# The delta rule's output gate: projected token tile by token tile from both halves of a side

## The reference

```python
def gated_deltanet_mixer(h, w_in, conv_w, a_log, dt_bias, out_norm, w_out):
    proj = h @ w_in                                     # [512, 1024] @ [1024, 4112]
    qkv = causal_depthwise_conv_silu(proj[..., :o1], conv_w)
    z = proj[..., o1:o2].reshape(b_sz, t_len, GDN_HEADS, GDN_DV)
    ...
    o = gated_delta_rule_chunked(q, k, v, g, beta).astype(h.dtype)
    o = rms_norm(o, out_norm) * jax.nn.silu(z)
    return o.reshape(b_sz, t_len, GDN_V_WIDTH) @ w_out
```

## Time and profile before

| | us |
|---|---|
| median of 3 runs | 2427.6 |
| lowest and highest | 2426.79, 2427.78 |
| the profiled execution | 2430.54 |
| its span in the trace | 2428.8 |

### The profile page before, as it was taken

The page is one execution under the profiler, slowest core; times in us unless marked ns, Lnnn a source line. Parts: engine busy times, 40 slices in busy tenths (PEclk is TensorE's granted clock), DMA queues, the critical chain, the costliest instruction groups (busy, mean ns, idle before and its releaser), DMA issues. The chain is left out here.

```text
span 2428.8 us, 26752 instructions
## 1 busy us (share of the span) xinstructions
PE 2238.0 (92%) x10932; PEld 1765.1 (73%) x10932; DVE 1128.3 (46%) x1668; ACT 811.1 (33%) x1147; POOL 138.3 (6%) x52
## 2 busy tenths in 40 slices
PE   6998899989999997999597899999899898999997
PEld 4885467868878875787495688888678566888885
DVE  2014765633254266876564544431552545544413
ACT  4311374333133154443133332221332653322211
POOL 3331000000000001310010000000000000000000
PEclk9997899999999998999688999999999999999998
DMA  3311002222223222232202223222234012222321
GB/s 126 104 57 53 1 1 70 96 81 93 99 75 105 87 70 72 72 109 92 65 23 70 69 87 104 87 95 96 69 105 156 1 53 70 89 102 87 104 87 52
DMA packets 43015, 190.22 MB, mean 78 GB/s; under 512 B 15808, under 2 KB 16512, under 8 KB 22032
## 3 DMA queue, kind: packets, MB, share of 16 engines
q1 hardware_dynamic: 40560, 184.32, 22.2%
q10 hardware_dynamic: 2336, 4.23, 0.5%
HBM read 184.80 MB, written 3.74 MB: 78 GB/s over the span
## 5 line engine op out<-in xcount | busy, mean ns | idle before, releaser
L422 PE MATMUL psum<-split,weights_high 128*128 128x512 f32 x1688 | 680.6, 403 | 54.1 <-DVE split L1160 19.5
L424 PE MATMUL psum<-split,weights_low 128*128 128x512 f32 x1688 | 676.1, 401 | 0.0
L423 PE MATMUL psum<-split,weights_high 128*128 128x512 f32 x1688 | 674.1, 399 | 0.0
L240 DVE TENSOR_TENSOR weights_low<-weights_raw,weights_high 128x2048 fp32r<-128x2048 f32 x139 | 318.6, 2292 | 563.9 <-ACT weights_high L213 563.8
L213 ACT CAST weights_high<-weights_raw 128x2048 fp32r<-128x2048 f32 x164 | 309.8, 1889 | 588.7 <-PE psum L424 580.9
L422 PEld LDWEIGHTS psum<-split,weights_high 128*128 128x128 f32 x1688 | 321.8, 191 | 139.7 <-issue 26.0
L423 PEld LDWEIGHTS psum<-split,weights_high 128*128 128x128 f32 x1688 | 322.0, 191 | 77.9
L424 PEld LDWEIGHTS psum<-split,weights_low 128*128 128x128 f32 x1688 | 321.1, 190 | 79.0 <-issue 0.2
L230 POOL TENSOR_TENSOR weights_low<-weights_raw,weights_high 128x2048 fp32r<-128x2048 f32 (+3 forms) x25 | 108.2, 4329 | 862.4 <-ACT weights_high L213 855.3
L424 PE MATMUL psum<-hidden,weights_low 128*128 128x512 f32 x352 | 140.4, 399 | 0.0
L423 PE MATMUL psum<-hidden,weights_high 128*128 128x512 f32 x352 | 138.7, 394 | 0.0
(11 more groups left out here) (406 smaller groups left out, 2703.2 us busy)
## 6 DMA issues: line engine op xcount, KB each, us to landing
weights_raw<-in_weights SPq DMA_DIRECT2D x161, 1024.0 KB, 4.8
minus_c<-minus_c_rows ACTq DMA_DIRECT2D x16, 256.0 KB, 7.5
x_stream<-in_x SPq DMA_DIRECT2D x2, 1024.0 KB, 7.9
gdn_in_grown<-gdn_rows SPq DMA_DIRECT2D x4, 512.0 KB, 4.5
gdn_chain_grown<-gdn_rows SPq DMA_DIRECT2D x4, 512.0 KB, 4.1
out<-x_stream SPq DMA_DIRECT2D x8, 256.0 KB, 2.1
rope_table<-rope_tables SPq DMA_DIRECT2D x1, 1024.0 KB, 5.3
weights_raw<-in_weights SPq DMA_DIRECT2D x1, 768.0 KB, 4.2
```

What stands on the lines that cost most here:

```text
L240: self.nc.vector.tensor_tensor(out=self.low[:, n % 2, 0:width], in0=self.raw[:, n % 2, 0:width], in1=self.high[:, n % 2, 0:width].bitcast( ...
L422: nc.tensor.matmul(bank, wh, ah, start=first, stop=False)
L423: nc.tensor.matmul(bank, wh, al, start=False, stop=False)
L424: return nc.tensor.matmul(bank, wl, ah, start=False, stop=last)
```

## The change

PE takes both chunks of a side together: it waits once for the second chunk's low part, and then runs the 24 matmuls of token tile 0, of tile 1, and so on. The number of matmuls, their operands and shapes stay. `products` counts two for each tile at its end, where it counted one for each half. ACT's `split_high` of +2 and +4 move from behind tile 0 to behind tile 3, with an explicit wait for the last tile. DVE's `split_low_vector` of +2 moves from behind tile 0 to behind the five solve steps of tile 3, right before that of +3.

```diff
             def gate_done(side, j):
-                return weights.tiles_before[z_chunk + 2 * side + 1] + j + 1
+                return weights.tiles_before[z_chunk + 2 * side] + 2 * (j + 1)
...
                         for side in range(2):
-                            for half in range(2):
-                                chunk = z_chunk + 2 * side + half
-                                pe.wait_ge(weights.low_ready, chunk + 1)
-                                parts = weights.parts(Chunk(chunk), 4)
-                                for j in range(TT):
-                                    if half == 0:
-                                        if side == 0:
-                                            pe.wait_ge(bank_free, n_tiles - 3 + j)
-                                        else:
-                                            pe.wait_ge(z_read, j + 1)
-                                    for k in range(4):
-                                        a = 4 * half + k
-                                        token = [split[:, n, a, j * P:(j + 1) * P] for n in range(2)]
-                                        last = product(psum[:, j, :], token, [p[:, k, :] for p in parts], a == 0, a == DT - 1)
-                                    last.then_inc(weights.products, 1)
+                            first = z_chunk + 2 * side
+                            pe.wait_ge(weights.low_ready, first + 2)
+                            for j in range(TT):
+                                if side == 0:
+                                    pe.wait_ge(bank_free, n_tiles - 3 + j)
+                                else:
+                                    pe.wait_ge(z_read, j + 1)
+                                for a in range(DT):
+                                    parts = weights.parts(Chunk(first + a // 4), 4)
+                                    token = [split[:, n, a, j * P:(j + 1) * P] for n in range(2)]
+                                    last = product(psum[:, j, :], token, [p[:, a % 4, :] for p in parts], a == 0, a == DT - 1)
+                                last.then_inc(weights.products, 2)
...
                                 nc.scalar.activation(tanh[:, o % 2, :], psum[:, j, :], ACT.Tanh, scale=0.5).then_inc(tanh_ready, 1)
-                                if j == 0:
-                                    weights.split_high(act, Chunk(z_chunk + 2 + 2 * side))
+                            act.wait_ge(weights.products, gate_done(side, TT - 1))
+                            weights.split_high(act, Chunk(z_chunk + 2 + 2 * side))
                             if side == 0:
                                 weights.split_high(act, Chunk(z_chunk + 3))
...
                                 if side == 0 and j == 0:
-                                    weights.split_low_vector(dve, z_chunk + 2)
                                     dve.wait_ge(col_pe, 3)
...
-                            weights.split_low_vector(dve, z_chunk + 3 + side)
+                            weights.split_low_vector(dve, z_chunk + 2 + 2 * side)
+                            if side == 0:
+                                weights.split_low_vector(dve, z_chunk + 3)
```

## The result

| | before | changed |
|---|---|---|
| median of 6 runs, us | 2427.69 (2426.79 to 2429.9) | 2439.02 (2437.0 to 2439.24) |
| profiled execution, us | 2430.54 | 2438.99 |
| its span, us | 2428.8 | 2437.0 |

The change makes the kernel slower: ratio 1.0042, 95% interval 1.0029 to 1.0055, that is +7.0 to +13.4 us. Timed again later it was 2436.96 against 2428.25 us, ratio 1.0032 (1.0021 to 1.0043), +8.7 us. Forecast were +5.4 us and 2430.4 to 2436.6 us. The sign was right, the size was not.

A forecast was written before the change was run, and what follows sets the result against it. DVE's queue was taken to set the stage's end. Start +4.1, turn +5.5, restarts -1.8, small terms -0.3 and tail -2.2 gave +5.3 (+5.4 by the stage's end), so 2433.0 us; range 2430.4 to 2436.6 us.

The forecast's parts named there:

- Bound of the kernel: Gate stage: DVE's queue up to the transposed copy's end sets the end, 1185.53 us before; PE does not.
- Step 1: Start of side 0: PE also waits for the second chunk's low part and starts 4.1 us later.
- Step 2: DVE in side 0: first tile 4.1 us earlier, at 1133.5; the gain is spent waiting for tiles.
- Step 3, the turn: Between the sides: PE stands 11.0 us for high parts, DVE's solves and two low parts; before, 2.49 + 2.99.
- Step 4: PE's side 1: 22.49 us of matmuls plus 1.9 for the restart, ending at 1185.3 against 1177.7 before.
- Step 5: Tail: high part, low part and copy end 5.65 us behind PE, 7.8 before; 2.2 us come back.
- What is not in the trace: When the clock rises later, in the next stage: taken as 0, with 1.5 us on either side.
- From the profile to the median: The stage's whole shift carried on to the median: 2427.6 + 5.4 = 2433.0 us, 0.22% more.
- B (faster): DVE's queue alone sets the end and its earlier start brings it 4.1 us forward: 2423.5 us; chance 0.03.
- A: Cheap restarts and a shorter low clock stretch next stage: +3.2 us, 2430.8, no change that can be told; chance 0.30.
- C: Restart after 11 us of rest takes much longer at 1.2 GHz: +8.1 us, 2435.7; chance 0.07.

The follow-up runs named there:

- pad_tail: The kernel before, with five more transposed copies of the solved blocks in DVE's tail: +6.8 us against before.
- solve_early: The kernel before, half by half, with 15 solve steps moved into DVE's idle time ahead of tile 0 and its other work reordered: -13.6 us against before.
- start_only: The kernel before, but PE waits for the second chunk's low part before starting side 0: +4.5 us against before.
- low_first: The changed kernel, but DVE makes the low parts of +2 and +3 ahead of tile 3's five solve steps: -0.3 us against before.

## Why the prediction was off

**Bound of the kernel: right.** DVE's queue set the stage's end; in pad_tail the stage paid for each copy, and solve_early got 16 us out of the stage by moving DVE's work alone.

**Step 1: right.** PE starts 4.21 us behind R2's transpose (1126.40 - 1122.19) where it was 0.11; forecast 4.1 later. start_only prices it at 4.0 in the stage.

**Step 2: right.** DVE's first tile came 12.4 us behind R2, forecast 12.5, after 8.24 us idle (forecast 8.3).

**Step 3, the turn: right**, 11.03 us for 11.0, ended by `weights_low`; and 4 of them are the solve steps, as low_first showed.

**Step 4: mis-sized.** The restart at the turn lost 2.7 us, not 1.9: from 1161.82 to ACT's tanh at 1187.19 are 25.37 us, where 22.49 + 0.16 are due. The first lost 1.8 (1126.40 to 1133.96, where 5.62 + 0.16 are due). I took the mean of three, though the trace had one of 2.7 behind the longest of its pauses within the gate, and the new one is its copy; 13 matmuls at 0.50, as in the earlier trace rows, although the pause was 11.03 us and not 2.99:

```profile
1161.82:1167.50 5.68, 5.68 (x13) 4.46 (x14) 0.00 (x0) 0.00 (x0) 0.00 (x0) 0.50 0.79 320
```

This is +0.8 us, and with -0.1 at the first restart it makes the stage's 6.1 from 5.4. Over four profiles of the changed kernel the stage costs 5.9. (A slip in the reading: the first restart of before has 8 slow matmuls, not about 10. Its loss of 1.6 us was taken from times and stands.)

**Step 5: right.** From ACT's last tanh to the copy's end 1192.84 - 1187.19 = 5.65 us, forecast 5.65.

**What is not in the trace: mis-sized.** I took 0 for the clock's behaviour in the recurrence, with 1.5 us either way. It was +0.7 against the usual 111.2 us of before, and +4.0 against the short kind; with the mean of before's seven, 110.8, it is +1.2. So by the profiles the change costs 5.9 + 1.2 + 0.1 behind = 7.2 us. That lies within my range: these two terms explain why 5.4 was too low, not why the measured time fell outside.

**From the profile to the median: this is the step that failed.** I set 2427.6 + 5.4 = 2433.0 us, as if three runs within 1 us gave the kernel's time, and had no term for how far executions of one kernel lie apart. R2's transpose starts anywhere within 4.5 us, whatever the kernel, and before's single runs spread over 8.5 us. The first measurement had +11.3. Of this 2.6 did not come again: the changed kernel's median of 6 was 2.1 above its later median of 8 (2439.02 and 2436.96), and before's 0.6 below its later one of 24 (2427.69 and 2428.25). So the small base was the lesser part; why the first six runs of the changed kernel were longer than its later ones is not known. What lies between 7.2 and the second measurement's 8.7 (5.1 to 10.4) is within its interval; between 7.2 and the first's (7.0 to 13.4) it just is. If before's timed runs took the short recurrence more often than its profiles, once in seven, part of the 1.5 us left would be that; no run shows it, and it stays open.

**The rivals.** B (faster) was out, for the reason given: both slots are held to the end of the side. A needed cheap restarts, and the one at the turn was dear. C came nearest in size, by a mechanism that did not occur: the restart behind the 11 us had no extra stretch at 0.50, and what came on top lay elsewhere.

## What to carry to other kernels

When two halves of a double-buffered operand are consumed together, neither slot comes free until both do: price the refill, in the order in which its engines' queues have it, as a full stop, and the lost head start of the first half as another. Look first for idle time in the queue of the engine that sets the end: a new order of DVE's work, with 11 us of solve steps moved into 12.4 us of waiting, was worth more than either order on PE. Before forecasting a difference of 0.2%, find out how far two executions of the same kernel lie apart, and in which stretch.

## What the hardware showed that was not expected

The gate's stretch of before, with its three restarts at the low clock, took 67.2 or 67.3 us in seven profiles, with the whole program shifted by up to 3.8 us ahead of it. A pause of 11.03 us cost the same restart as one of 2.99 us, 13 matmuls at 0.50. An unchanged sequence of 111 us takes 108.0 to 112.0 us, the long times where the clock is low for longer in it (47.8 us instead of 41.0 or 44.4), and not by its mean clock alone: the changed kernel's had 0.77 and was longer than before's with 0.76. Which low stretch hits which chain in it stays open.
